# A hybrid decoder trunk in split fp32: the common product routine reads its moving operand in lines of 16 columns, last line first

## The chip, the cores and the metric

The kernel runs on one core of a Trainium2 chip. The metric is the device time of one execution in microseconds (us); lower is better. The time before is 2354.65 us, the median of three runs.

## The reference, cut to what matters

Two decoder layers over x (512 tokens by 1024 features, fp32), each a SwiGLU feed-forward block (1024 to 2 x 2816 and back), a token mixer with attention over 256 memory tokens, and a second feed-forward block. Most of the arithmetic is in plain products:

```python
def swiglu_ffn(h, w_in, w_out):
    gate, up = jnp.split(h @ w_in, 2, axis=-1)
    return (jax.nn.silu(gate) * up) @ w_out
...
for i in range(DEPTH):
    x = x + 0.5 * swiglu_ffn(rmsnorm(x, ffn1_norm[i]), ffn1_w_in[i], ffn1_w_out[i])
    h = rmsnorm(x, mix_norm[i])
    mk, mv = jnp.split(mem_n @ mem_w_kv[i], 2, axis=-1)
    ...
    z = h @ hgrn_w_in[j]          # layer 0; gmlp_w_in in layer 1
    ...
    x = x + jnp.concatenate([o_mix, o_mem], axis=-1) @ w_out
    x = x + 0.5 * swiglu_ffn(rmsnorm(x, ffn2_norm[i]), ffn2_w_in[i], ffn2_w_out[i])
return rmsnorm(x, final_norm)
```

## The kernel before, in words

Activations lie with features on the 128 partitions and the 512 tokens along the free dimension. Each product is cut into units. A unit takes a weight block of up to eight 128x128 tiles, and the same number of activation blocks of 128x512, and accumulates them into one bank of PSUM (acc0 to acc3, taken in turn; each is 512 fp32 columns). For the keys of the memory the activation blocks and the results are 256 columns wide.

Every fp32 operand x is split into a rounded part hi and a remainder lo, both of type fp32r. ScalarE rounds a loaded weight block into w_hi (L1528), VectorE subtracts to get w_lo (L1255). A product is then three matmuls in the same bank: w_hi with hi (L1093), w_hi with lo (L1094), w_lo with hi (L1095). The weight tile is the stationary operand, the activation block the moving one. All of this is in the routine `unit`, which waits once for its weights, issues its 24 (or 18) matmuls, and attaches the semaphore unit_done to the last. VectorE reads a bank when its unit is done (L1381 and others), and SyncE loads the next weight block of that lane into the buffer that the unit has freed.

The first stage (two sets of keys and values of the memory) is followed by twelve phases. All of them except part of the memory stage (values, L1137 to L1139), part of the gated MLP (L846 to L848) and the last product (L262 to L264) go through `unit`. Those three places have their own matmuls, with the roles swapped: the weights are the moving operand. Attention scores, the recurrence and the transposes have their own matmuls too and write to the banks mix0 to mix3. Loops over quads of units run as hardware loops; within them the addresses of the operands of `unit` are constants, only the counts waited for change.

In every matmul of `unit` the moving operand and the bank are given as plain stretches of 512 (or 256) adjacent fp32 columns.

Of the kernel before, what the change touches and what calls it, by code (L numbers as in the profile page):

```python
# [67 lines left out]
class Phase:  # L68
# [11 lines left out]
    @property  # L80
    def end_quad(self):
        return self.q0 + self.units // LANES


def hybrid_trunk(nc, a, out):
# [34 lines left out]
    with ExitStack() as ctx:  # L120
# [21 lines left out]
        def lane_of(buffer, q, j):  # L142

            at = KU * P * j + (KV_SHIFT if type(q) is int and q < kv.end_quad else 0)
            return buffer[:, at:at + KU * P].rearrange("p (k c) -> p k c", c=P)
# [899 lines left out]
        def _(pe):  # L1045
# [8 lines left out]
            for mb in range(MB):  # L1054
                pe.wait_ge(sem(f"mem_loaded{mb}"), 16)
                for kb in (0, 4, 1, 5, 2, 6, 3, 7):
                    m = pe.transpose(mix[kb % 4][:, (kb // 4) * MEM + mb * P:(kb // 4) * MEM + (mb + 1) * P],
                                     mem_raw[:, mb, kb * P:(kb + 1) * P], ident[:])
# [26 lines left out]
            def unit(q, j, operands, bank, start, stop, each=None):  # L1085

                pe.wait_ge(w_lo_ready, LANES * q + j + 1)
                last = len(operands) - 1
                top, rest = lane_of(w_hi, q, j), lane_of(w_lo, q, j)
                for i, (hi, lo) in enumerate(operands):  # L1090
                    if each:
                        each(i)
                    pe.matmul(bank, top[:, i, :], hi, start=(start and i == 0), stop=False)  # L1093
                    pe.matmul(bank, top[:, i, :], lo, start=False, stop=False)  # L1094
                    m = pe.matmul(bank, rest[:, i, :], hi, start=False, stop=(stop and i == last))  # L1095
                m.then_inc(unit_done, 1)


# [5 lines left out]
            def k_quad(it):  # L1104
                turn, first = kv_turn_of(it), it == 0
                for j in range(LANES):
                    if first and j == 2:
                        pe.wait_ge(sem("vecs_ready"), 1)
                    if first and j == 3:
                        pe.wait_ge(sem("vecs_ready"), 2)  # L1110
                    if not first:
                        if KV_QUADS[it - 1] == "k":
                            pe.wait_ge(acc_read, LANES * turn + j - 3)
                        else:
                            pe.wait_ge(sem("v_staged"), LANES * kv_turn_of(it - 1) + j + 1)
                    unit(it, j, mem_parts, acc[j][:, 0:MEM], True, True, mem_block if first and j == 0 else None)
                    if first and j == 1:
                        turn_vectors()
                    if 2 <= LANES * it + j < DB + 2:
                        turn_x(LANES * it + j - 2)  # L1120
# [28 lines left out]
            def in_unit(ph, s, it, j, first=False):  # L1149

                def each(i):
                    pe.wait_ge(h_lo_ready, DB * s + i + 1)
                if first and s == 0:
                    pe.wait_ge(sem("v_staged"), 4 * LANES - 3 + j)
                pe.wait_ge(acc_read, ph.g0 + LANES * it + j - 3)
                unit(ph.q0 + it, j, h_parts, acc[j][:], True, True, each if first and j == 0 else None)
                if first and j == 0:
                    pe.wait_ge(sq_sum_ready, DB * (s + 1))
                    pe.matmul(mix[3][:], ones[:], sq_sum, start=True, stop=True).then_inc(ss_done, 1)

            s = n_ffn = 0
            for i, (kind, ph) in enumerate(phases):
# [18 lines left out]
                elif kind == "gmlp_in":  # L1181
# [14 lines left out]
                    def u_unit(it, j):  # L1196
                        if type(it) is int and it == 0:
                            pe.wait_ge(sem("v_gelu"), 3 * TB + j + 1)
                        else:
                            pe.wait_ge(acc_read, ph.g0 + 2 * XH + LANES * it + j - 3)  # L1200
                        unit(ph.q0 + 6 + it, j, h_parts, acc[j][:], True, True)
# [641 lines left out]
```

## Time and profile before

| | |
|---|---|
| median of 3 runs (lowest, highest) | 2354.65 us (2350.22, 2355.73) |
| the profiled execution, its own time | 2353.23 us |
| its span, first to last instruction | 2351.5 us |
| granted TensorE clock, mean | 0.997 of full speed |
| matmul records | 11040 |
| TensorE busy | 2328.8 us of the span |
| VectorE, ScalarE, GpSimd busy | 1233.5, 764.4, 264.5 us |

Matmuls are pipelined: a record's duration overlaps the next one's, and its end is modelled. What a matmul costs in a dense stretch is the distance between the starts of two neighbours, not its duration. A group in the list of instructions gives line, engine, operation, output and inputs, shapes and count, then busy time, mean duration in ns, and idle time of the engine before them with what ended it.

### The profile page before, as it was taken

The numbers are of one execution on the slowest core, as the hardware profiler recorded it, in microseconds if no ns is written. First come the engines' busy times: TensorE is split into PE (matmuls) and PEld (weight loads), VectorE is DVE, ScalarE is ACT, GpSimd is POOL, SyncE is SP. The second block draws the span as 40 slices with busy tenths as digits, with TensorE's granted clock in tenths as the row PEclk, the third lists the DMA queues.
The fourth block names the chain that finished last, engine by engine and source line by source line (L and its number), as shares of the span: only waits on it lengthen the run. The fifth ranks groups of instructions, "written<-read, shape, count | busy, mean of one in ns | idle before, by whom it ended". The sixth has DMA issues, their size and how long they took to land.

```text
span 2351.5 us, 29800 instructions
## 1 busy us (share of the span) xinstructions
PE 2328.8 (99%) x11040; PEld 1947.6 (83%) x11040; DVE 1233.5 (52%) x1467; ACT 764.4 (33%) x1045; POOL 264.5 (11%) x236
## 2 busy tenths in 40 slices
PE   9999999999999999999999999999999999999998
PEld 9988888878888888888878888888888888888887
DVE  6654443467888654444445444336437644444422
ACT  4432222244445322222222222224433222222322
POOL 3400001111333420000110000120001212000000
PEclk9999999999999999999999999999999999999999
DMA  7733333332222333333333333333232233333322
GB/s 235 215 98 95 93 97 99 95 104 69 72 71 80 99 97 92 97 98 98 98 90 90 98 98 98 97 92 107 72 99 85 86 98 99 99 98 97 92 95 92
DMA packets 400693, 234.35 MB, mean 100 GB/s; under 512 B 7692, under 2 KB 386672, under 8 KB 400624
## 3 DMA queue, kind: packets, MB, share of 16 engines
q1 hardware_dynamic: 397328, 223.37, 32.1%
q0 software_dynamic: 3280, 10.02, 1.2%
q8 instruction: 47, 0.77, 0.1%
q14 instruction: 22, 0.18, 0.0%
q10 hardware_dynamic: 16, 0.00, 0.0%
HBM read 227.07 MB, written 6.29 MB: 99 GB/s over the span
## 4 chain that ended last, share of the span: by engine, by line
PE 92%; DVE 4%; ACT 2%; issue 1%; DMA 1%; POOL 0%; DVEq 0%; ACTq 0%; SPq 0%; POOLq 0%
PE acc L1093 26%; PE acc L1094 26%; PE acc L1095 26%; PE acc L847 1%; PE acc L846 1%; PE acc L848 1%; ACT w_hi L1528 1%; DVE w_lo L1255 1%; PE acc L262 1%; PE acc L264 1%; PE acc L263 1%; PE mix L264 1%; PE mix L262 1%; PE mix L263 1%; DMA raw<-in_mem_w_kv_dram 1%
## 5 line engine op out<-in xcount | busy, mean ns | idle before, releaser
L1255 DVE TENSOR_TENSOR w_lo<-raw,w_hi 128x1024 fp32r<-128x1024 f32 (+1 forms) x422 | 544.9, 1294 | 636.2 <-ACT w_hi L1528 623.1
L1093 PE MATMUL acc<-h_hi,w_hi 128*128 128x512 f32 x1920 | 756.0, 394 | 7.6 <-DVE h_lo L1318 5.3
L1094 PE MATMUL acc<-h_lo,w_hi 128*128 128x512 f32 x1920 | 748.5, 390 | 0.0
L1095 PE MATMUL acc<-h_hi,w_lo 128*128 128x512 f32 x1920 | 748.4, 390 | 0.0
L1528 ACT ACTIVATE w_hi<-raw 128x1024 fp32r<-128x1024 f32 (+1 forms) x422 | 436.4, 1038 | 341.7 <-DMA raw<-in_ffn_w_out_dram 219.6
L1093 PEld LDWEIGHTS acc<-h_hi,w_hi 128*128 128x128 f32 x1920 | 361.5, 188 | 84.4 <-DVE h_lo L1318 6.6
L1094 PEld LDWEIGHTS acc<-h_lo,w_hi 128*128 128x128 f32 x1920 | 361.5, 188 | 75.4 <-issue 2.0
L1095 PEld LDWEIGHTS acc<-h_hi,w_lo 128*128 128x128 f32 x1920 | 361.2, 188 | 75.4
L1093 PE MATMUL acc<-act_hi,w_hi 128*128 128x512 f32 (+1 forms) x976 | 367.6, 377 | 1.9 <-DVE w_lo L1255 1.2
L1095 PE MATMUL acc<-act_hi,w_lo 128*128 128x512 f32 (+1 forms) x976 | 365.7, 375 | 0.0
L1094 PE MATMUL acc<-act_lo,w_hi 128*128 128x512 f32 (+1 forms) x976 | 365.7, 375 | 0.0
L1381 DVE TENSOR_TENSOR tmp<-acc,rstd 128x512 f32<-128x512 f32 x176 | 121.7, 691 | 202.2 <-PE acc L1095 201.9
L1093 PEld LDWEIGHTS acc<-act_hi,w_hi 128*128 128x128 f32 x976 | 183.2, 188 | 36.0 <-DVE w_lo L1255 1.4
L1095 PEld LDWEIGHTS acc<-act_hi,w_lo 128*128 128x128 f32 x976 | 183.3, 188 | 33.2
L1094 PEld LDWEIGHTS acc<-act_lo,w_hi 128*128 128x128 f32 x976 | 183.5, 188 | 32.7
L1600 ACT ACTIVATE act_hi<-tmp 128x512 f32 (+1 forms) x88 | 55.6, 632 | 404.3 <-DVE tmp L1387 404.3
L1751 POOL TENSOR_TENSOR sq<-x 128x512 f32 (+1 forms) x48 | 57.6, 1201 | 1131.3 <-DVE x L1478 1130.7
L1596 ACT ACTIVATE tmp<-tmp 128x512 f32<-128x512 f32 x88 | 55.6, 632 | 255.5 <-DVE tmp L1381 255.5
L1550 ACT ACTIVATE h_hi<-tmp 128x512 fp32r<-128x512 f32 (+1 forms) x48 | 30.4, 632 | 200.7 <-DVE tmp L1314 200.7
L1392 DVE TENSOR_TENSOR act_lo<-tmp,act_hi 128x512 f32 (+1 forms) x88 | 60.6, 689 | 40.1 <-ACT act_hi L1600 40.1
L1753 POOL TENSOR_TENSOR sq<-sq 128x512 f32<-128x512 f32 x48 | 78.3, 1631 | 3.8
L1387 DVE TENSOR_TENSOR tmp<-tmp 128x512 f32<-128x512 f32 x88 | 60.9, 692 | 10.7
(243 smaller groups left out, 1895.0 us busy)
## 6 DMA issues: line engine op xcount, KB each, us to landing
raw<-in_ffn_w_in_dram SPq DMA_DIRECT2D x176, 512.0 KB, 3.7
raw<-in_ffn_w_out_dram SPq DMA_DIRECT2D x70, 512.0 KB, 3.4
raw<-in_hgrn_w_in_dram SPq DMA_DIRECT2D x40, 512.0 KB, 3.7
raw<-in_gmlp_w_in_dram SPq DMA_DIRECT2D x40, 512.0 KB, 3.6
raw<-in_mem_w_kv_dram SPq DMA_DIRECT2D x32, 512.0 KB, 4.4
raw<-in_gmlp_w_out_dram SPq DMA_DIRECT2D x24, 512.0 KB, 3.4
raw<-in_ffn_w_out_dram SPq DMA_DIRECT2D x24, 384.0 KB, 3.0
raw<-in_hgrn_w_out_dram SPq DMA_DIRECT2D x16, 512.0 KB, 3.4
```

Source lines behind the costliest of these rows:

```text
L1093: pe.matmul(bank, top[:, i, :], hi, start=(start and i == 0), stop=False)
L1094: pe.matmul(bank, top[:, i, :], lo, start=False, stop=False)
L1095: m = pe.matmul(bank, rest[:, i, :], hi, start=False, stop=(stop and i == last))
L1255: dve.tensor_tensor(lane_of(w_lo, q, j)[:, 0:nkb], lane_of(raw, q, j)[:, 0:nkb], f32(lane_of(w_hi, q, j)[:, 0:nkb]), ALU.subtract).then_in ...
L1381: dve.tensor_tensor(tmp[:, j, :], acc[j][:], rstd[:], ALU.mult).then_inc(acc_read, 1)
L1387: dve.tensor_tensor(tmp[:, j, :], tmp[:, j, :], tmp[:, j - 1, :], ALU.mult).then_inc(prod_done, 1)
L1392: dve.tensor_tensor(act_lo[:, f, :], tmp[:, j, :], f32(act_hi[:, f, :]), ALU.subtract).then_inc(act_lo_ready, 1)
L1528: act.activation(lane_of(w_hi, q, j)[:, 0:nkb], lane_of(raw, q, j)[:, 0:nkb], ACT.Copy).then_inc(w_hi_ready, 1)
L1596: act.activation(tmp[:, j, :], tmp[:, j, :], ACT.Silu).then_inc(silu_done, 1)
L1600: act.activation(act_hi[:, 2 * it + j // 2, :], tmp[:, j, :], ACT.Copy).then_inc(act_hi_ready, 1)
L1751: pool.tensor_tensor(sq_one, x[:, m_, :], x[:, m_, :], ALU.mult).then_inc(sq_ready, 1)
L1753: pool.tensor_tensor(sq_sum, sq_sum, sq_one, ALU.add).then_inc(sq_sum_ready, 1)
```

## The change

A view over the columns is added, and the three matmuls of `unit` take the bank and the moving operand through it. The view cuts the free dimension into lines of 16 columns (64 bytes) and goes through the lines from the last to the first; within a line the columns are taken in ascending order. Input and output are turned alike, so every column of the result lands where it did. The stationary operands, the number of instructions, the waits and increments, and all other lines are as before.

```diff
+LINE = 16
+
+
+def lines_down(view):
+
+    return view.rearrange("p (l c) -> p l c", c=LINE)[:, ::-1, :]
...
                     if each:
                         each(i)
-                    pe.matmul(bank, top[:, i, :], hi, start=(start and i == 0), stop=False)
-                    pe.matmul(bank, top[:, i, :], lo, start=False, stop=False)
-                    m = pe.matmul(bank, rest[:, i, :], hi, start=False, stop=(stop and i == last))
+                    pe.matmul(lines_down(bank), top[:, i, :], lines_down(hi), start=(start and i == 0), stop=False)
+                    pe.matmul(lines_down(bank), top[:, i, :], lines_down(lo), start=False, stop=False)
+                    m = pe.matmul(lines_down(bank), rest[:, i, :], lines_down(hi), start=False,
+                                  stop=(stop and i == last))
                 m.then_inc(unit_done, 1)
```

## Rows read from the trace of the kernel before

**Rows 1.** The page, busy time of each engine, share of the span and instructions.

```profile
PE 2328.8 (99%) x11040; PEld 1947.6 (83%) x11040; DVE 1233.5 (52%) x1467; ACT 764.4 (33%) x1045; POOL 264.5 (11%) x236
```

**Rows 2.** The page, the chain that ended last, shares of the span.

```profile
PE 92%; DVE 4%; ACT 2%; issue 1%; DMA 1%; POOL 0%; DVEq 0%; ACTq 0%; SPq 0%; POOLq 0%
```

**Rows 3.** Groups of instructions by shape, the matmuls of the common routine.

```profile
L1093 PE MATMUL acc<-h_hi,w_hi 128*128 128x512 f32 x1920 | 756.0, 394 | 7.6 <-DVE h_lo L1318 5.3 <-DVE w_lo L1255 2.3
...
L1093 PE MATMUL acc<-act_hi,w_hi 128*128 128x512 f32 x848 | 330.8, 390 | 0.3 <-DVE act_lo L640 0.3
...
L1093 PE MATMUL acc<-act_hi,w_hi 128*128 128x256 f32 x128 | 36.9, 288 | 1.6 <-DVE w_lo L1255 1.2 <-DVE act_lo L1267 0.5
```

**Rows 4.** Two dense stretches: start and end, length, busy time and records by engine.

```profile
core 0: us, PE busy (x) PEld busy (x) DVE busy (x) ACT busy (x) POOL busy (x), PEclk, DMA share, GB/s
860.00:1200.00 340.00, 340.00 (x1500) 281.17 (x1499) 155.46 (x170) 95.25 (x116) 13.64 (x12) 1.00 0.32 95
1900.00:2200.00 300.00, 300.00 (x1323) 248.05 (x1323) 145.14 (x159) 86.05 (x105) 23.02 (x17) 1.00 0.34 98
```

**Rows 5.** Timeline of PE, first and last of 26 neighbouring 512-column matmuls.

```profile
300.10 0.39 PE L1093 MATMUL acc<-h_hi,w_hi 128*128 128x512 f32 x1
...
305.77 0.39 PE L1094 MATMUL acc<-h_lo,w_hi 128*128 128x512 f32 x1
```

**Rows 6.** Timeline of PE, first and last of 19 neighbouring 256-column matmuls.

```profile
31.86 0.28 PE L1093 MATMUL acc<-act_hi,w_hi 128*128 128x256 f32 x1
...
33.98 0.28 PE L1093 MATMUL acc<-act_hi,w_hi 128*128 128x256 f32 x1
```

**Rows 7.** Groups by shape, VectorE: operands read in rows, and in one stretch.

```profile
L1387 DVE TENSOR_TENSOR tmp<-tmp 128x512 f32<-128x512 f32 x88 | 60.9, 692 | 10.7
...
L928 DVE SCALAR_TENSOR_TENSOR tmp<-mix,vecs,q_row 128x512 f32<-128x512 f32 x16 | 12.0, 751 | 2.1 <-PE mix L913 0.7 <-DVE q_row L923 0.2
...
L625 DVE SCALAR_TENSOR_TENSOR tmp<-mix,vecs,tmp 128x512 f32<-128x512 f32 x8 | 5.9, 743 | 3.9 <-ACT tmp L696 3.9
...
L677 DVE TENSOR_TENSOR tmp<-work 128x512 f32<-128x512 f32 x8 | 5.5, 692 | 0.3
```

**Rows 8.** Groups by shape, ScalarE: results written in four lines, and in one stretch.

```profile
L861 ACT ACTIVATE work<-acc,small 128x512 f32<-128x512 f32 x16 | 10.8, 688 | 11.6 <-PE acc L848 11.6
...
L693 ACT ACTIVATE tmp<-mix,small 128x512 f32<-128x512 f32 x8 | 5.4, 669 | 3.7 <-PE mix L611 3.7
...
L338 ACT ACTIVATE out_rows<-mix 128x512 f32<-128x512 f32 x8 | 4.8, 598 | 32.0 <-PE mix L272 32.0
L711 ACT ACTIVATE work<-mix 128x512 f32<-128x512 f32 x8 | 4.7, 591 | 1.1 <-PE mix L584 1.1
```

**Rows 9.** Timeline of PE, the four records of two plain fp32 products.

```profile
1605.25 1.88 PE L802 MATMUL mix<-pair,ones 128*128 128x512 f32 x4
```

**Rows 10.** Groups by shape, the same four records.

```profile
L802 PE MATMUL mix<-pair,ones 128*128 128x512 f32 x4 | 1.9, 592 | 0.0
```

**Rows 11.** Groups by shape, the splits of a weight block.

```profile
L1528 ACT ACTIVATE w_hi<-raw 128x1024 fp32r<-128x1024 f32 x398 | 416.2, 1049 | 262.4 <-DMA raw<-in_ffn_w_out_dram 140.4 <-DMA raw<-in_gmlp_w_out_dram 44.4 <-DMA raw<-in_gmlp_w_in_dram 33.3
...
L1255 DVE TENSOR_TENSOR w_lo<-raw,w_hi 128x1024 fp32r<-128x1024 f32 x398 | 515.5, 1298 | 560.6 <-ACT w_hi L1528 547.5 <-DMA v_scratch<-tmp 6.5
```

**Rows 12.** The page, DMA issues: count, size, median us from issue to landing.

```profile
raw<-in_ffn_w_in_dram SPq DMA_DIRECT2D x176, 512.0 KB, 3.7
```

## The prediction, on record before the result was known

> **What bounds the kernel now.** I read the page first: TensorE is busy for 2328.8 of 2351.5 us, no other engine for more than 52% [rows 1]. A busy share alone says little of pipelined matmuls, so the chain that ended last comes next: it is TensorE for 92% [rows 2], and the idle time in front of the matmuls of the changed routine is 7.6 us at its largest group [rows 3]. Other engines' durations matter only where they would make TensorE wait, and they hardly do.
>
> Then I asked what one matmul costs. Two stretches of 340 and 300 us are wholly busy and hold 1500 and 1323 records: 340.00/1500 = 226.7 ns and 300.00/1323 = 226.8 ns each [rows 4]. The timeline says the same for neighbours: (305.77 - 300.10)/25 = 226.8 ns [rows 5]. The granted clock there is 1.00, the level of 2.4 GHz [rows 4], at which 512 columns, one a cycle, last 213.3 ns. So 13.3 ns of each matmul are something else. The 256-column matmuls stand (33.98 - 31.86)/18 = 117.8 ns apart [rows 6], 11.1 ns more than their columns (106.7). The kernel is a stream of matmuls at nearly one column a cycle; what the change does to that stream is the whole question.
>
> **The size of the lever.** Each of L1093, L1094 and L1095 runs 1920 + 848 times at 512 columns and 128 times at 256 [rows 3]: 8304 wide and 384 narrow matmuls are changed. The wide ones are 8304 x 226.7 ns = 1882 us, 80% of the span, the narrow ones 384 x 117.8 ns = 45 us. Every nanosecond on a changed matmul is 8.7 us of the total. A measurement of this kernel tells about 0.3% (7.1 us) from no change, and that is 0.8 ns a matmul. There is hardly room between nothing and plainly visible.
>
> **The change, part by part.**
>
> Instructions, waits, semaphores, DMAs: none is added, moved or removed. Nothing new can be queued behind a wait. The addresses within the hardware loops are constants before and after, so no register work is added. Cost 0, exactly.
>
> Order of the columns: each matmul of a group writes its columns in the same turned order, so a column is added to 512 columns after it was last written, as before. unit_done still comes with the last column. Readers of a bank see no difference. Cost 0. If it were not hidden, one late unit_done would show as idle time of VectorE, which idles half of the time anyway.
>
> Line turns: this is the unknown price. A wide matmul now makes 31 turns from the end of one line of 16 to the start of the line before it, in its reads and in its writes; a narrow one makes 15. No matmul of the trace reads or writes its columns in pieces, so I bound a turn by other engines' rows.
> - VectorE, reading. L677 reads one operand in eight rows (the last column of each chunk, repeated 64 times, then on to the next chunk). It takes 692 ns, L1387 without such rows 692 ns [rows 7]. Seven turns cost 0 within 1 ns.
> - VectorE, reading backwards. L928 reads q_row four times over, three jumps back by 127 columns: 751 ns against 743 ns for L625 with the same kind of operation [rows 7]. At most 8/3 = 2.7 ns a turn.
> - ScalarE, writing. L338 writes four lines that lie 1024 columns apart: 598 ns against 591 ns for L711 [rows 8], 2.3 ns a turn. L861 writes four lines likewise: 688 ns against 669 ns for L693 [rows 8], 6.3 ns a turn; but the function differs (Gelu, Ln), so this is the loosest bound.
>
> The lower end is 0. The upper is 6.3 ns a turn: 31 x 6.3 = 195 ns on a wide matmul, 8304 x 195 ns = 1619 us, and 384 x 15 x 6.3 ns = 36 us, in sum 1655 us. I take 0. L677 is the cleanest pair (same engine, same operation, most turns), and the differences of the others are as small as those between unlike operations. A further reason is that each line is whole: 16 adjacent columns of 64 bytes each time, so no piece is fetched twice.
>
> Here two rules of the Trainium skill pull apart. The row on the turn is L677, 692 ns with seven turns and 692 ns without [rows 7]. The Trainium skill, PSUM — Partial Sum Buffer, Specifications (TRN2), states flatly that "any non-contiguous AP slows matmuls significantly". By that rule the sum would be far from 0 (below, as a rival). The Trainium skill, Vector Engine (DVE) Microarchitecture Reference, Measured stream behaviour on trn2, says of VectorE that between runs of at least two adjacent aligned words any hop is free; carried over to TensorE, the sum is 0. L677 agrees with the second, and no row of this trace tests the first.
>
> Below nothing: the order of the lines could only gain what is not columns, 13.3 ns wide and 11.1 ns narrow. I see no reason why it should, but no row excludes it.
>
> **Sum.** 0 + 0 + 0 on the profiled execution's span of 2351.5 us. 1.7 us lie around the span (its own time is 2353.23 us), and the median of the three runs is 1.4 us above that. I forecast 2355 us, the median unchanged.
>
> **The rivals.**
> 1. A turn costs one TensorE cycle, 0.417 ns at 2.4 GHz. A wide matmul grows by 31 x 0.417 = 12.9 ns to 239.6 ns, a narrow one by 6.3 ns: 8304 x 12.9 + 384 x 6.3 ns = 107 + 2 = 110 us, so 2464 us. It decides from 0.03 ns a turn on, as 31 of these make the 0.8 ns above. For it: the stream has no slack in its columns, and a turn is new to it. Against it: L677.
> 2. A turn costs two cycles: +219 us, 2574 us. For it are the 2.3 and 2.7 ns of L338 and L928; against it the same row as before.
> 3. One cost per matmul, not per turn: it starts at the far end of its operand. At the 2.7 ns of one backward jump this is 8688 x 2.7 ns = 23 us, 2378 us. Against it: the transition between matmuls already jumps between tiles, and all of them stand 226.7 ns apart [rows 4].
> 4. The broken pattern halves the rate of the columns. A wide matmul grows by 213.3 ns, a narrow one by 106.7 ns: 1771 + 41 = 1812 us, so 4167 us, near the upper bound above. This is what the flat rule of the PSUM page would come to. Against it: the lines are whole runs of 16, not single columns.
> 5. The other side: faster. The 13.3 ns might come from the way columns are fetched. The plain fp32 products of L802 speak for that: four records take 1.88 us from the first start to the last end [rows 9], one of them is given 592 ns [rows 10], so the starts are (1.88 - 0.592)/3 = 0.429 us apart. At two cycles a column 512 columns last 0.427 us, so only 2.7 ns are left over there. If the new order removed all of the excess: 8304 x 13.3 + 384 x 11.1 ns = 115 us, 2240 us. It decides from 0.8 ns a matmul. A wide unit of 24 matmuls would still last 5.12 us, more than its block's landing (3.7 us) [rows 12], its rounding (1.05 us) or its subtraction (1.30 us) [rows 11], so no other engine would take the gain back. Against it: the spacing is the same in 340 us over all lanes and blocks [rows 4], so it doesn't look like something that depends on addresses.
> The "change does nothing" case is the forecast itself; if the two dimensions were merged away somewhere it would look the same, but a reversed order of lines cannot be merged.
>
> **How the numbers follow.** Forecast (0 a turn, within 0.8 ns a matmul) 0.62; rival 1 0.13; rival 2 0.07; rival 3 0.05; rival 4 0.06; rival 5 0.07. Slower is 0.13 + 0.07 + 0.05 + 0.06 = 0.31, faster 0.07, same 0.62. The forecast's own range is 2347 to 2362 us. To leave out no more than 0.20 the range must reach to rival 1 and may drop rivals 2, 4 and 5: 2346 to 2468 us.
>
> **What would show it.** In the profile after, the same two stretches of the timeline: starts 226.7 ns apart (right), 239.6 (rival 1), 252.5 (rival 2), 229.4 (rival 3), 440 (rival 4), 213.3 (rival 5). The narrow ones tell a cost per turn from one per matmul: per turn their growth is 15/31 of the wide ones', per matmul it is the same. The matmuls of L846 to L848 and L262 to L264 are unchanged and must keep 226.7 ns; if they move too, the cause is not the pattern. The prediction is wrong if a turn has any regular price at all, however small.

## The result, and the profile after

The kernel became slower: 2400.53 us (median of 4 runs, 2399.26 to 2402.12) against 2354.08 us (4 runs beside it). The ratio is 1.020, with a 95% interval of 1.0182 to 1.0218. That is 46 us more. It lies inside the stated range of 2346 to 2468 us, but the forecast itself was "no change" (2355 us, its own range up to 2362 us) with a chance of 0.62; slower had 0.31.

The page of the changed kernel, busy time of each engine, then the chain that ended last:

```profile
PE 2378.2 (99%) x11040; PEld 1947.9 (81%) x11040; DVE 1232.9 (51%) x1467; ACT 763.2 (32%) x1045; POOL 262.4 (11%) x236
...
PE 94%; DVE 3%; ACT 1%; issue 1%; DMA 1%; POOL 0%; DVEq 0%; ACTq 0%; SPq 0%; POOLq 0%
```

Against [rows 1, 2]: the same 11040 matmul records, and TensorE is busy for 49.4 us more, while VectorE, ScalarE and GpSimd are busy as long as before. The span grew by 47.8 us (2351.5 to 2399.3). So no new wait shows, and the matmuls themselves take longer.

The same two stretches of time as in [rows 4], of the changed kernel:

```profile
core 0: us, PE busy (x) PEld busy (x) DVE busy (x) ACT busy (x) POOL busy (x), PEclk, DMA share, GB/s
860.00:1200.00 340.00, 340.00 (x1457) 273.64 (x1456) 160.61 (x176) 94.89 (x117) 22.00 (x17) 1.00 0.32 94
1900.00:2200.00 300.00, 300.00 (x1294) 241.72 (x1294) 137.67 (x151) 80.80 (x98) 26.20 (x20) 1.00 0.32 95
```

Both are still wholly busy at a granted clock of 1.00 (the 2.4 GHz level), but they hold 1457 and 1294 records in place of 1500 and 1323. 340.00/1457 = 233.4 ns against 226.7. The timeline of PE, two wide matmuls of the changed routine and two narrow ones, first and last of 25 and of 19 neighbours:

```profile
300.13 0.40 PE L1101 MATMUL acc<-h_hi,w_hi 128*128 128x512 f32 x1
...
305.73 0.40 PE L1101 MATMUL acc<-h_hi,w_hi 128*128 128x512 f32 x1
```

```profile
31.91 0.28 PE L1101 MATMUL acc<-act_hi,w_hi 128*128 128x256 f32 x1
...
34.03 0.28 PE L1101 MATMUL acc<-act_hi,w_hi 128*128 128x256 f32 x1
```

Wide: (305.73 - 300.13)/24 = 233.3 ns, 6.67 ns more than 226.7; at 2.4 GHz that is 16 cycles for 512 columns. Narrow: (34.03 - 31.91)/18 = 117.8 ns, the same as in [rows 6] (over all narrow ones the mean durations in the groups by shape are 1 to 2 ns longer, 281 against 279 ns for w_lo with act_hi).

One group of changed matmuls and one of unchanged ones, by shape:

```profile
L1101 PE MATMUL acc<-h_hi,w_hi 128*128 128x512 f32 x1920 | 769.5, 401 | 6.0 <-DVE h_lo L1327 3.8 <-DVE w_lo L1264 2.3
...
L855 PE MATMUL acc<-w_lo,h_hi 128*128 128x512 f32 x128 | 49.8, 389 | 0.0
```

L1101 (L1093 before) rose from a mean of 394 ns [rows 3] to 401 ns. L855, the gated MLP's own product with the plain pattern, has the 389 ns that it had before (as L847), and the starts of L854 to L856 stand 226.8 ns apart on average, before and after. The cost belongs to the pattern.

**Why 48 us of span and not 55.** 8304 x 6.67 ns would be 55 us. The loss is smaller where other matmuls or pauses come in between. The stage of the recurrence (from one L1159 to the next, before) and the feed-forward stage after it:

```profile
480.05:866.90 386.85, 382.83 (x1955) 320.37 (x1954) 291.19 (x330) 169.03 (x267) 99.62 (x77) 1.00 0.28 84
866.90:1229.20 362.30, 360.22 (x1587) 297.60 (x1586) 166.67 (x182) 100.13 (x123) 20.95 (x17) 1.00 0.33 96
```

and the same stages of the changed kernel:

```profile
490.40:882.40 392.00, 389.05 (x1955) 320.29 (x1954) 291.13 (x331) 169.29 (x268) 100.03 (x78) 1.00 0.28 83
882.40:1254.70 372.30, 370.74 (x1587) 298.10 (x1586) 166.68 (x182) 99.90 (x123) 20.88 (x17) 1.00 0.32 93
```

The feed-forward stage has 1584 changed matmuls. TensorE's busy time grew by 10.52 us (360.22 to 370.74), 6.6 ns each, nearly the full price. The recurrence stage has 1344 (56 units of 24), and its busy time grew by only 6.22 us, its length by 5.15 us, where the full price would be 9.0 us. The starts in the trace show two reasons. The smaller one is seen before the change, after an interruption by the recurrence's short matmuls (L605):

```profile
593.94 0.40 PE L1094 MATMUL acc<-h_lo,w_hi 128*128 128x512 f32 x1
...
594.87 0.39 PE L1095 MATMUL acc<-h_hi,w_lo 128*128 128x512 f32 x1
```

These are the first and last of five neighbours: (594.87 - 593.94)/4 = 232 ns, not 226.7. The plain stream runs unevenly (224 to 236 ns) for some ten matmuls after each interruption before it settles: over the 42 interruptions of the stage the second to tenth distances are 229.2 ns on average, from the eleventh or twelfth on 226.7. After the change, at the same place:

```profile
604.76 0.40 PE L1102 MATMUL acc<-h_lo,w_hi 128*128 128x512 f32 x1
...
605.69 0.40 PE L1103 MATMUL acc<-h_hi,w_lo 128*128 128x512 f32 x1
```

(605.69 - 604.76)/4 = 232 ns as well, within the timeline's 0.01 us. Over the 42 interruptions the second to tenth distances are now 233.4 ns on average, no more than later ones. So right after an interruption the change costs some 4 ns a matmul and not 6.67. Over the stage, the mean distance of neighbouring changed matmuls rose from 229.4 to 235.3 ns, by 5.8 ns, which is 1.1 us less than the full price.

The larger reason is pauses. Distances of over 0.6 us between two starts of TensorE sum to 6.8 us (five) before and to 4.1 us (three) after in this stage: what the slower matmuls lose, the waits give back in part. 9.0 - 1.1 - 2.7 = 5.2 us, as measured. Over the whole kernel the mean distance rose from 227.7 to 234.1 ns (8304 x 6.4 ns = 53 us), and such pauses fell from 23.3 to 18.1 us; 53 - 5 = 48 us. Why the pauses are shorter was not followed up one by one.

### The profile page after: what moved, and what is told of

Same layout as the page of the kernel before. It is cut to its first block, busy times and chain, and to the rows that moved or that the text cites. A ratio compares the mean times of both kernels' runs of the same rounds, so it can differ in the third digit from the quotient of the medians.

```text
span 2399.3 us, 29800 instructions
## 1 busy us (share of the span) xinstructions
PE 2378.2 (99%) x11040; PEld 1947.9 (81%) x11040; DVE 1232.9 (51%) x1467; ACT 763.2 (32%) x1045; POOL 262.4 (11%) x236
## 4 chain that ended last, share of the span: by engine, by line
PE 94%; DVE 3%; ACT 1%; issue 1%; DMA 1%; POOL 0%; DVEq 0%; ACTq 0%; SPq 0%; POOLq 0%
PE acc L1101 26%; PE acc L1102 26%; PE acc L1103 26%; PE acc L854 1%; PE acc L855 1%; PE acc L856 1%; PE acc L270 1%; PE acc L272 1%; PE acc L271 1%; PE mix L272 1%; PE mix L270 1%; PE mix L271 1%; ACT w_hi L1537 1%; DVE w_lo L1264 1%; DMA raw<-in_mem_w_kv_dram 1%
## 5 line engine op out<-in xcount | busy, mean ns | idle before, releaser
L1101 PE MATMUL acc<-h_hi,w_hi 128*128 128x512 f32 x1920 | 769.5, 401 | 6.0 <-DVE h_lo L1327 3.8
L1103 PE MATMUL acc<-h_hi,w_lo 128*128 128x512 f32 x1920 | 763.7, 398 | 0.0
L1102 PE MATMUL acc<-h_lo,w_hi 128*128 128x512 f32 x1920 | 763.6, 398 | 0.0
L1101 PEld LDWEIGHTS acc<-h_hi,w_hi 128*128 128x128 f32 x1920 | 361.5, 188 | 93.6 <-DVE h_lo L1327 5.1
L1101 PE MATMUL acc<-act_hi,w_hi 128*128 128x512 f32 (+1 forms) x976 | 374.7, 384 | 2.7 <-DVE act_lo L1276 1.6
L1103 PE MATMUL acc<-act_hi,w_lo 128*128 128x512 f32 (+1 forms) x976 | 373.0, 382 | 0.0
L1102 PE MATMUL acc<-act_lo,w_hi 128*128 128x512 f32 (+1 forms) x976 | 372.9, 382 | 0.0
L1390 DVE TENSOR_TENSOR tmp<-acc,rstd 128x512 f32<-128x512 f32 x176 | 121.7, 691 | 229.9 <-PE acc L1103 229.8
L1101 PEld LDWEIGHTS acc<-act_hi,w_hi 128*128 128x128 f32 x976 | 183.5, 188 | 41.8 <-DVE w_lo L1264 2.5
```

Source lines behind the costliest of these rows:

```text
L1101: pe.matmul(lines_down(bank), top[:, i, :], lines_down(hi), start=(start and i == 0), stop=False)
L1102: pe.matmul(lines_down(bank), top[:, i, :], lines_down(lo), start=False, stop=False)
L1103: m = pe.matmul(lines_down(bank), rest[:, i, :], lines_down(hi), start=False, stop=(stop and i == last))
L1390: dve.tensor_tensor(tmp[:, j, :], acc[j][:], rstd[:], ALU.mult).then_inc(acc_read, 1)
```

## The experiments

All edits are against the changed kernel, but for the one on no new memory touched, which is against the kernel before. The measure is the spacing of wide matmuls in a dense stretch. Where one order holds for a whole kernel it is read from the stretch from 860 to 1200 us, as above: 1500 records are 226.7 ns, 1457 are 233.4 ns.

**Which side pays.** Two kernels, each with the turned order on one side only.

```diff
-pe.matmul(lines_down(bank), top[:, i, :], lines_down(hi), ...)
+pe.matmul(bank, top[:, i, :], lines_down(hi), ...)
```

> Only the moving operand is taken in lines of 16, last first; the bank is written in plain ascending order (so the token columns of every product of the routine come out permuted, and the output is not the reference's). In the changed kernel wide matmuls of the routine start 233.3 ns apart against 226.7 before. Theory A, the turns cost on the reading side: 233.3 ns here too, time about 2400 us. Theory B, they cost on the PSUM side: 226.7 ns, 2354 us. Theory C, both sides pay a part and the parts add: between, about 230 ns and 2377 us.

2400.6 us, ratio 1.0197 (1.018 to 1.0214):

```profile
860.00:1200.00 340.00, 340.00 (x1457) 273.62 (x1456) 160.15 (x176) 94.94 (x118) 22.00 (x17) 1.00 0.32 94
```

```diff
-pe.matmul(lines_down(bank), top[:, i, :], lines_down(hi), ...)
+pe.matmul(lines_down(bank), top[:, i, :], hi, ...)
```

> Only the bank is written in lines of 16, last first; the moving operand is read in plain order (the columns come out permuted, the output is not the reference's). Theory A, the reading side pays: 226.7 ns between starts, 2354 us. Theory B, the PSUM side pays: 233.3 ns, 2400 us. Theory C, both pay a part: about 230 ns, 2377 us. If both this and the run with the reads alone show 233.3 ns, the two sides' costs overlap and do not add.

2353.42 us, ratio 0.9999 (0.9989 to 1.0008):

```profile
860.00:1200.00 340.00, 340.00 (x1500) 281.17 (x1499) 155.06 (x170) 95.23 (x116) 13.61 (x11) 1.00 0.32 95
```

Theory A of both: the whole cost is on the reading side. Writing a bank of PSUM in lines of 16, last first, with 31 turns and accumulation in it, costs nothing that can be told (0.0011 of the time is 0.3 ns a matmul).

**Direction.** Lines of 16, ascending, even ones first.

```diff
-    return view.rearrange("p (l c) -> p l c", c=LINE)[:, ::-1, :]
+    return view.rearrange("p (l two c) -> p two l c", two=2, c=LINE)
```

> Lines of 16 again on both sides, but ascending: the even lines first, then the odd ones. 30 jumps forward over one line and one back. Theory A, any jump between lines of 16 costs, whatever its direction: 233.3 ns, 2400 us. Theory B, only going backwards costs: 226.7 ns or at most a cycle more, 2354 us. A dimension more in the access pattern might cost by itself: then over 233.3 ns.

2454.4 us, ratio 1.0424 (1.0407 to 1.0442). The timeline of PE, first and last of 13 neighbours:

```profile
1000.12 0.41 PE L1101 MATMUL acc<-h_hi,w_hi 128*128 128x512 f32 x1
...
1003.00 0.41 PE L1101 MATMUL acc<-h_hi,w_hi 128*128 128x512 f32 x1
```

(1003.00 - 1000.12)/12 = 240.0 ns, 13.3 ns above plain, twice the cost of the backward order. Neither theory A nor B had that: going backwards is not the trouble. The third possibility named, that a further dimension of the pattern costs by itself, was left by this run; the last run below has the same three dimensions in one lane and is at 226.7 ns, so it falls too.

**Number of turns.** The changed kernel with `LINE = 256`, 32, 8 and 4 in place of 16.

> Lines of 256 columns, last first: one turn in a wide matmul instead of 31, none in a narrow one. Theory A, a price for each turn (6.67 ns over 31 turns is 0.215 ns, about half a TensorE cycle): 226.9 ns, 2355 us, no difference that can be told. Theory B, a price for each matmul whose pattern is not one plain stretch, or that starts at the far end (6.67 ns once): 233.3 ns, 2400 us.

> Lines of 32 columns, last first: 15 turns in a wide matmul, 7 in a narrow one. Theory A, each turn has a price (0.215 ns, from 6.67 ns over 31 turns): 226.7 + 3.2 = 229.9 ns between starts, 27 us more than before, 2381 us. Theory B, memory is read in rows of 16 columns (64 bytes), entering a row costs about one cycle in plain order (32 rows make the 13.3 ns that plain order has over its columns) and half a cycle more when it is entered from the row after it: also 229.9 ns. Theory C, a threshold (up to 32 columns a turn is hidden): 226.7 ns, 2354 us.

> Lines of 8 columns, last first: 63 turns, but only 31 of them lead from one row of 16 columns to the row before it. Theory A, a price for each turn: 226.7 + 63 x 0.215 = 240.2 ns, 2354 + 8304 x 13.5 ns = 2466 us. Theory B, only the change of the row of 16 counts: 233.3 ns, as with lines of 16, 2400 us.

> Lines of 4 columns, last first: 127 turns, 31 changes of a row of 16. Theory A, a price for each turn: 226.7 + 27.3 = 254.0 ns, about 2581 us. Theory B, rows of 16 alone: 233.3 ns, 2400 us. If rows are smaller than 16 columns this or the run with lines of 8 shows it by a step: a row of 8 would first show here as no further rise.

The stretch from 860 to 1200 us, of the kernels with lines of 256, 32, 8 and 4 in this order:

```profile
860.00:1200.00 340.00, 340.00 (x1500) 281.17 (x1499) 156.54 (x171) 95.98 (x117) 16.48 (x13) 1.00 0.33 96
```

```profile
860.00:1200.00 340.00, 340.00 (x1457) 273.35 (x1456) 159.93 (x175) 95.33 (x117) 20.97 (x17) 1.00 0.32 94
```

```profile
860.00:1200.00 340.00, 340.00 (x1457) 273.46 (x1456) 160.62 (x176) 94.96 (x117) 22.03 (x17) 1.00 0.32 93
```

```profile
860.00:1200.00 340.00, 340.00 (x1457) 273.61 (x1457) 160.62 (x176) 94.94 (x117) 21.98 (x17) 1.00 0.32 93
```

| lines of | turns | time, us | ratio (95%) | ns between starts |
|---|---|---|---|---|
| 256 | 1 | 2355.47 | 1.0001 (0.9992 to 1.0011) | 226.7 |
| 32 | 15 | 2395.33 | 1.0179 (1.0162 to 1.0196) | 233.4 |
| 16 (the change) | 31 | 2400.53 | 1.020 (1.0182 to 1.0218) | 233.4 |
| 8 | 63 | 2402.12 | 1.0208 (1.0191 to 1.0225) | 233.4 |
| 4 | 127 | 2402.24 (one run) | | 233.4 |

A price for each turn is dead: 15 turns cost as much as 127. One turn costs nothing that can be told, so it is no price for a pattern with two dimensions either. It is a step. All three theories of lines of 32 fail: two asked for 229.9 ns there (a price for each turn, a price for rows of 16 columns), the third, that turns are hidden up to 32 columns, for 226.7.

The time with lines of 32 is 5 us below that with lines of 16. In the stretch shown the spacing is the same, but over three of the other stages it is 232.4 to 232.6 ns on average in place of 233.3 to 233.4. Why is not known.

**No new memory touched.** The moving operand is the first 16 columns, read 32 times; the bank is written in plain order.

```diff
+    n = view.shape[1] // LINE
+    return view[:, 0:LINE].rearrange("p (o c) -> p o c", o=1).to_broadcast([P, n, LINE])
```

> The bank is written in plain order, and the moving operand is its first 16 columns, read 32 times over (the routine's products are those of 16 tokens only, the output is not the reference's). 31 jumps back by 15 columns, all inside one piece of 64 bytes. Theory A, each jump back has a price: 233.3 ns or so. Theory B, entering a row of 16 columns is what costs: no row is entered, so the 13.3 ns of plain order go as well, 213.3 to 216 ns, and the kernel loses up to 8304 x 13.3 ns = 110 us, to 2244 us. Theory C, the 13.3 ns are paid between matmuls for another reason, and jumps inside a row are free: 226.7 ns, 2354 us.

```profile
860.00:1200.00 340.00, 340.00 (x1407) 266.71 (x1406) 145.21 (x160) 89.35 (x110) 11.81 (x9) 1.00 0.31 90
```

340.00/1407 = 241.7 ns, and 2468.07 us (one run): the dearest of all, where theory B wanted the cheapest; none of the three theories had it. Staying in the same 64 bytes is worse than any walk through memory that was tried. That pointed away from a price for going somewhere and towards one for where consecutive lines lie.

**Is it the weights that are loaded beside?** Two kernels, with a variant for each lane of a quad. In the first, most matmuls load 64 or 32 weight columns and not 128:

```diff
+                    if j == 0:
...
+                        pe.matmul(bank[0:64], top[:, i, 0:64], lo, start=False, stop=False)
...
+                    elif j == 1:
...
+                        pe.matmul(lines_down(bank[0:64]), top[:, i, 0:64], lines_down(lo), start=False, stop=False)
```

> In every unit the matmuls between the first and the last take only the first 64 columns of the weight tile (units of lanes 0 and 1) or the first 32 (lanes 2 and 3), so that only the first 64 or 32 output rows are summed over all blocks and the output is not the reference's. Lanes 0 and 2 read the moving operand plainly, lanes 1 and 3 in lines of 16, last first. The number of moving columns is 512 throughout. Theory W, the loading of the next weights and the moving columns get in each other's way at the memory: both the 13.3 ns that plain order has over its columns and the 6.7 ns of the lines shrink with the weight tile: lane 0 about 220 ns, lane 1 about 223 ns, lane 2 about 217 ns, lane 3 about 218 ns. Theory M, the moving operand pays alone, whatever is loaded beside it: 226.7, 233.3, 226.7 and 233.3 ns. Mixed: the 13.3 ns go and the 6.7 ns stay, or the other way round.

The timeline of PE, the first matmul of five units in a row (lane 3, 0, 1, 2, 3). Each lies 24 matmuls behind the one above:

```profile
1002.18 0.40 PE L1133 MATMUL acc<-h_hi,w_hi 128*128 128x512 f32 x1
...
1007.78 0.39 PE L1103 MATMUL acc<-h_hi,w_hi 128*128 128x512 f32 x1
...
1013.29 0.40 PE L1113 MATMUL acc<-h_hi,w_hi 128*128 128x512 f32 x1
...
1018.89 0.40 PE L1123 MATMUL acc<-h_hi,w_hi 128*128 128x512 f32 x1
...
1024.45 0.40 PE L1133 MATMUL acc<-h_hi,w_hi 128*128 128x512 f32 x1
```

Lined, 32 weight columns (lane 3): 5.60 us/24 = 233.3 ns. Plain, 64 (lane 0): 5.51/24 = 229.6. Lined, 64 (lane 1): 5.60/24 = 233.3. Plain, 32 (lane 2): 5.56/24 = 231.7 ns. Theory W in its simple form falls: with a quarter of the weights to load, neither the 233.3 ns of the lined order nor the 226.7 ns of the plain one falls. Theory M (the moving operand pays alone) has the lined lanes right and not the plain ones, which get dearer. That is not the uneven start after another lane: the plain lanes stay uneven (224 to 236 ns) through all 24 matmuls of a unit.

In the second, the weight buffers of each lane lie elsewhere, and all else is as in the change. The line that moves them:

```diff
-            at = KU * P * j + (KV_SHIFT if type(q) is int and q < kv.end_quad else 0)
+            at = KU * P * j + (0, 16, 32, 64)[j]
```

> The changed kernel, with the weight buffers of lanes 0 to 3 shifted by 0, 16, 32 and 64 columns (64, 128 and 256 bytes) against where they lie now; nothing else differs and the output is the reference's. Theory W, weight loads and moving reads collide by address: the spacing differs between lanes, somewhere away from 233.3 ns. Theory M, the moving operand pays alone, or the collisions do not depend on such an offset: 233.3 ns in all lanes.

The timeline of PE, the first matmul of the units of lanes 2, 3, 0, 1 and 2:

```profile
1004.05 0.40 PE L1110 MATMUL acc<-h_hi,w_hi 128*128 128x512 f32 x1
...
1009.73 0.40 PE L1114 MATMUL acc<-h_hi,w_hi 128*128 128x512 f32 x1
...
1015.33 0.40 PE L1102 MATMUL acc<-h_hi,w_hi 128*128 128x512 f32 x1
...
1020.92 0.40 PE L1106 MATMUL acc<-h_hi,w_hi 128*128 128x512 f32 x1
...
1026.53 0.40 PE L1110 MATMUL acc<-h_hi,w_hi 128*128 128x512 f32 x1
```

Lane 2, shifted by 32 columns: 5.68/24 = 236.7 ns. Lanes 3, 0 and 1 (64, 0, 16 columns): 5.60, 5.59 and 5.61 us, 233 to 234 ns. So where the weights lie does have a part in it, in one of three shifts. The time was 2409.94 us (one run). That the two reads of TensorE meet by their addresses would fit both answers, but it is not shown: the shift also moves what DMA, ScalarE and VectorE write into these buffers.

**Which orders are free.** Again a variant for each lane.

```diff
+lines_64, lines_128 = lines_down_of(64), lines_down_of(128)
...
+def swapped(view):
+    return view.rearrange("p (l two c) -> p l two c", two=2, c=LINE)[:, :, ::-1, :]
...
+def backwards(view):
+    return view[:, ::-1]
```

> The four lanes of a quad read and write in four different orders: lane 0 in lines of 64, last first (7 turns), lane 1 in lines of 128, last first (3 turns), lane 2 in lines of 16 with each pair of neighbours swapped (16 steps back, 15 steps forward over two lines), lane 3 column by column from the last to the first. Known so far: lines of 256 226.7 ns, lines of 32, 16, 8 and 4 233.3 ns on average, even lines before odd ones 240 ns. Theory S, there is a step, not a price for each turn: 233.3 ns for both lane 0 and lane 1 or 226.7 ns for both, or one of each. Theory A', a price for each turn up to a ceiling of 6.67 ns, reached at 15 turns: lane 0 226.7 + 3.1 = 229.8 ns, lane 1 228.0 ns. Lane 2 under either: 233 to 240 ns. Lane 3: 233.3 ns if a piece of 4 or more adjacent columns fetched upward is not needed, far more (up to 440 ns) if it is.

The timeline of PE, the first matmul of the units of lanes 0, 1, 2, 3 and 0:

```profile
1003.68 0.40 PE L1117 MATMUL acc<-h_hi,w_hi 128*128 128x512 f32 x1
...
1009.13 0.39 PE L1121 MATMUL acc<-h_hi,w_hi 128*128 128x512 f32 x1
...
1014.57 0.40 PE L1125 MATMUL acc<-h_hi,w_hi 128*128 128x512 f32 x1
...
1020.18 0.40 PE L1129 MATMUL acc<-h_hi,w_hi 128*128 128x512 f32 x1
...
1025.78 0.40 PE L1117 MATMUL acc<-h_hi,w_hi 128*128 128x512 f32 x1
```

Lines of 64 last first: 5.45/24 = 227.1 ns. Lines of 128: 5.44/24 = 226.7. Pairs of 16 swapped: 5.61/24 = 233.8. Column by column backwards: 5.60/24 = 233.3 ns. The step lies between lines of 64 and lines of 32. Swapping neighbours inside a block of 64 is enough to pay it, and 512 columns fully backwards cost no more. Of the theories, the step (S) holds; the price for each turn up to a ceiling (A'), which asked for 229.8 and 228.0 ns in lanes 0 and 1, fails.

I then had one rule that fitted all of the orders, which the last run was made to break: within each block of 64 columns (256 bytes, counted from the operand's first column) the order must be the plain one; the order of the blocks is free.

```diff
+def even_odd_64(view):
+    return view.rearrange("p (l two c) -> p two l c", two=2, c=64)
...
+def by_quarter(view):
+    return view.rearrange("p (l four c) -> p four l c", four=4, c=LINE)
...
+def by_half(view):
+    return view.rearrange("p (l two c) -> p two l c", two=2, c=32)
```

> Four lanes, four orders, all ascending within a line. Lane 0: blocks of 64 columns, the even ones, then the odd ones. Lane 1: lines of 16, first the first quarter of all eight blocks of 64, then the second quarters, and so on. Lane 2: lines of 32, first the first halves of all blocks, then the second halves. Lane 3: plain. Theory R, the order inside each block of 64 columns (256 bytes) is what counts, and jumps between whole blocks are free in any direction: lane 0 and lane 3 226.7 ns; lane 1 at least the 240 ns that even lines before odd ones took; lane 2 between 233 and 240 ns. Theory J, long jumps forward are what made even lines before odd ones dearer than the backward ones: lane 0 above 226.7 ns too, and the longer jumps of lanes 1 and 2 (48 and 32 columns skipped) dearer in the order of their number, lane 1 above lane 2.

The timeline of PE, the first matmul of the units of lanes 2, 3, 0, 1 and 2:

```profile
1000.74 0.40 PE L1122 MATMUL acc<-h_hi,w_hi 128*128 128x512 f32 x1
...
1006.42 0.39 PE L1126 MATMUL acc<-h_hi,w_hi 128*128 128x512 f32 x1
...
1011.90 0.39 PE L1114 MATMUL acc<-h_hi,w_hi 128*128 128x512 f32 x1
...
1017.34 0.40 PE L1118 MATMUL acc<-h_hi,w_hi 128*128 128x512 f32 x1
...
1023.08 0.40 PE L1122 MATMUL acc<-h_hi,w_hi 128*128 128x512 f32 x1
```

Lane 0, whole blocks in even-odd order: 5.44/24 = 226.7 ns, free, though it jumps forward like the order that cost 13.3 ns. Lane 1, by quarters: 5.74/24 = 239.2 ns, just under the "at least 240" foretold. Lane 2, by halves: 5.68/24 = 236.7 ns, in the interval foretold. Lane 3, plain: 5.48/24 = 228.3 ns, a little above plain because it follows a lane with another order and settles late, as after the interruptions above (226.7 ns from its tenth matmul on). Theory J (long jumps forward cost) is refuted by lane 0. Theory R holds in what is free and what costs; it does not give the sizes, and its 240 for lane 1 was a little high.

One rival of theory R stands untested. Every free order here has runs of at least 64 adjacent columns, and every dear one has runs of at most 32. So the length of the run may be what counts, and not where the blocks begin. Runs of 64 that begin 32 columns further on would tell the two apart; nor was the moving operand itself ever shifted.

No experiment was faster than the kernel before.

## Why the prediction was right or wrong

**What bounds the kernel: right.** The forecast said that every nanosecond on a changed matmul is 8.7 us. The distances of the wide ones grew by 6.4 ns on average, 53 us in sum; 49.4 us came in busy time and 47.8 us in span. The forecast left out that shorter pauses would give 5 us back. No other engine moved.

**Instructions, waits, order of accumulation, unit_done: right.** The writes alone, with all of these in place, gave a ratio of 0.9999.

**Line turns, cost 0: wrong.** This is the step that failed. I took the term from VectorE's L677 [rows 7], and put the question as a price for a turn. Both were mistakes. The bound on a single turn was kept (6.67 ns over 31 turns is 0.215 ns, between 0 and 6.3), but there is no price for a turn. Measured: 0 for 1, 3 or 7 turns between blocks of 64, and 6.67 ns for 15 to 511 turns inside them, last first. Orders that come back to each block later cost 10.0 ns (by halves), 12.5 ns (by quarters) and 13.3 ns (even lines of 16, then odd ones).

That the range of 2346 to 2468 us held is luck. It reached that far only to take in rival 1, one cycle a turn, and that mechanism is refuted; 2400.5 us was not the value of the forecast or of any rival. A row of another engine could not show this. L677 takes 692 ns for its 512 columns, the moving operand is read in 226.7, and L677's seven jumps lead from one chunk of 64 columns to the next, which is free here too. Within a chunk L677 takes one column 64 times over, so it never changes the order inside a block.

**The rivals.** One cycle a turn (2464 us) had the right sign and was twice too large. Two cycles a turn (2574 us) was four times too large. The price for each matmul (2378 us) had the right sign and was too small: 2.7 ns was taken, 6.67 ns measured, and lines of 256 show that it is not paid by the matmul as such. Half rate was far off. Of the faster rival, the 13.3 ns over the columns in plain order remain in every order tried.

**The narrow matmuls** were to tell a price for each turn from one for each matmul. They did neither: 117.8 ns before and after. Why they hide it is not shown. The narrow matmuls of L1137 to L1139, with the plain order, also stand near 118 ns apart. The weight loads may set this pace. In a stretch that is nearly all narrow matmuls of both kinds they are busy almost without a break, before and then after:

```profile
30.00:60.00 30.00, 30.00 (x257) 29.80 (x256) 21.38 (x33) 15.62 (x21) 9.51 (x12) 1.00 0.66 201
```

```profile
30.00:60.00 30.00, 30.00 (x256) 29.70 (x256) 21.54 (x33) 15.62 (x21) 9.76 (x12) 1.00 0.66 206
```

PEld is busy for 29.80 and 29.70 of 30.00 us here, 116 ns a load, against 281.17 of 340.00 us in the stretch of wide ones [rows 4]. No run has tested it.

**The rules that were weighed.** Writing in lines left the time unchanged, and reading in whole blocks of 64 likewise. The Trainium skill, PSUM — Partial Sum Buffer, Specifications (TRN2), says that any non-contiguous pattern slows matmuls significantly: for the side it speaks of, the writes to PSUM, the measurement says no for lines of 16 columns (ratio 0.9999 with 31 turns). It gives no size; the half rate of rival 4 was mine. The free hop between runs of at least two adjacent aligned words, which the Trainium skill, Vector Engine (DVE) Microarchitecture Reference, Measured stream behaviour on trn2, gives for VectorE, does not carry over to TensorE's moving operand: lines of 16 columns cost 6.67 ns in 226.7. Nor did L677 bear it out, as the prediction says, since it reads a single column again and again and not runs of adjacent ones.

**What stays open.** Why 64 columns, whether the place of the blocks or the length of the run counts, and what makes the dear orders differ. The offset of the weight buffer changed one lane from 233.3 to 236.7 ns, and the load of fewer weights changed the plain lanes; so the stationary side takes part, but how is not shown. Nor is it shown where the 13.3 ns of plain order come from.

## What to carry to other kernels

Where a kernel is a dense stream of wide fp32r matmuls, read the moving operand in whole, ascending blocks of 64 columns, counted from its first column; blocks may come in the orders tried here at no cost. The output may be written in lines of 16, last first, at no cost that can be told; finer orders were not tried on the writing side alone. For an unknown price on the bounding engine, don't take the value from another engine's row only because that pair is clean: ask whether its jumps are of the same kind and its rate the same. And before one writes "so much a turn", the form of the law deserves a rival of its own; a step and a slope need different kernels to be told apart.

## What the runs showed of the hardware

- The mean spacing of 512-column fp32r matmuls with 128 weight columns was 226.7 ns for plain order and whole blocks of 64, 233.3 for all orders last first inside them, 236.7 by halves, 239.2 by quarters and 240.0 for even lines before odd ones. At 2.4 GHz 226.7, 233.3, 236.7 and 240.0 ns are 544, 560, 568 and 576 cycles, that is 32, 48, 56 and 64 over the 512 columns.
- Reading the same 16 columns again and again was the slowest of all orders, 241.7 ns.
- After an interruption by other matmuls the plain stream needs some ten matmuls to come back to 226.7 ns (229.2 ns on average until then, over 42 interruptions); the lined stream is at 233.3 ns from the third on.
- Fewer weight columns made the plain stream slower: 229.6 ns with 64, 231.7 ns with 32, against 226.7 with 128. The lined stream stayed at 233.3 ns with either.
- Moving the weight buffers by 32 columns changed the lined stream from 233.3 to 236.7 ns; moving them by 16 or 64 did not.
